# The residual h goes straight into the output, and the last rows are added to it by accumulating transfers from GpSimd

## The chip, the core and the metric

The kernel runs on one core of a Trainium2 chip. The metric is the time of one execution on the device in microseconds. Three runs of the kernel before gave 2551.84, 2552.77 and 2554.0 us, median 2552.77 us. The profiled execution has a span of 2550.6 us from its first to its last instruction.

Engine names in the rows are those of the profiler: PE is TensorE (PEld its weight loads), DVE is VectorE, ACT is ScalarE, POOL is GpSimd, SP is SyncE. ACTq is ScalarE's own issuing of transfers.

## The reference, cut to what matters

One layer of a decoder over 512 prompt rows and 64 sample rows, with D_MODEL = 2048:

```
xn = rmsnorm(x, n_mix_pre);  mix = mixer(xn)          # GLA and SSD heads, one output projection
h  = x + rmsnorm(mix, n_mix_post)
xn = rmsnorm(h, n_ffn_pre);  f = conv_ffn(xn)         # FFN_DIM = 5632, causal depthwise conv, silu gate
y  = h + rmsnorm(f, n_ffn_post)
```

All is float32. The outputs are y and the recurrent and convolution states. Only the last line is touched by the change: how h is kept from its making to the final addition, and who adds it.

## The kernel before, in words

Data are held with the model dimension on the partitions: 2048 features are KT = 16 tiles of 128, and a tile has T = 576 columns (512 prompt rows and 64 sample rows). Many steps work on half a tile, HALF = 288 columns; n = 0 and n = 1 name the halves. Nothing is scheduled by a library: every engine has its own program, written out in order, and waits on semaphores. An instruction that waits holds everything behind it on its engine.

Three stages matter here.

**Making h.** At about 940 to 980 us GpSimd adds x to the normalised mixer output (`add_x`, L555), and ScalarE scales and squares the result (`h_high`, L1006 and L1009). In the second half (n = 1), after every second tile, ScalarE issues one transfer of two tiles of h to the DRAM tensor `h_spill` (L1011, 8 transfers of 576 KB). VectorE waits for all of them (L2652) before it normalises h in place. In the down projection ScalarE issues one load of all of h (4608 KB) back into `x_hi` (L1255), at 2370.8 us.

**The last sums.** The down projection runs over five chunks of the FFN dimension; the last (`last_down`) gives 32 half tiles, first the 16 of n = 0 and then the 16 of n = 1. VectorE adds each to `acc` (`take_last`, L2775). ScalarE squares it (L1272) into a ring of four buffers, and the squares are summed over the tiles by two engines, tiles 1, 3, 4, 6, 7, 9, 10, 12 by GpSimd (`square_sum`, L579) and 5, 8, 11, 13, 14 by VectorE (L2795). The square of tile kt waits for the sum of tile kt-4. When all sums of a half are done, TensorE adds across partitions (`tokens_squared`, L1906), ScalarE takes the root (L1260, L1262), VectorE the reciprocal (L2446, L2448), and TensorE spreads it over the partitions (`roots_to_rows`, L1914).

**The last rows.** VectorE multiplies each half tile by its norm (`y_of`, L2784): those of n = 0 between the takes of n = 1, from 2519.4 us, and those of n = 1 after 2536.7 us. Then h is added, in SBUF: by VectorE for three tiles of n = 0 and five of n = 1 (`VE_ADDS`, L2787), by GpSimd for the other 24 half tiles (`add_h`, L586). ScalarE issues the stores to `yT` (`rows_out`, L1284), four for n = 0 and five for n = 1, seven of 576 KB and two of 288 KB. In its program they all stand behind the second root. At the end it waits for the nine stores (`y_st`, 144 = 9 x 16).

Of the kernel before, what the change touches and what calls it, by code (L numbers as in the profile page):

```python
# [30 lines left out]
F32 = mybir.dt.float32  # L31
F32R = mybir.dt.float32r
U8 = mybir.dt.uint8
ALU = mybir.AluOpType
# [3 lines left out]
P = 128  # L38
# [3 lines left out]
T = SEQ + SMP  # L42
KT = D // P
# [66 lines left out]
    _n += _w  # L110
NVEC = _n
MASK_TRI, MASK_TRI_S = 8, 9
VE_ADDS = ((7, 11, 15), (3, 7, 11, 14, 15))
POOL_SUMS, VE_SUMS = (1, 3, 4, 6, 7, 9, 10, 12), (5, 8, 11, 13, 14)

PADW = SC - 1 + SEQ + BATCHES * (SC - 1 + DEC)
# [13 lines left out]
def build(nc, xT, weights, vecs, ident_d, masks_d, gate2, sconv_in, fconv_in, fvec_d, gla_in,  # L130
          ssdT_in, ssd_in, yT, gla_p, ssd_p, sconv_out, fconv_out, gla_s, ssd_s):
    y_spill = nc.dram_tensor("y_spill", [2, 8, P, T], F32, kind="Internal").ap()
    spill = nc.dram_tensor("spill", [BESIDE, P, T], F32, kind="Internal").ap()
    h_spill = nc.dram_tensor("h_spill", [KT, P, T], F32, kind="Internal").ap()
    g_spill = nc.dram_tensor("g_spill", [FT, P, T], F32, kind="Internal").ap()
    with ExitStack() as ctx:
        def sb(name, shape, dt=F32):
# [2 lines left out]
        def sem(name):  # L140
            return ctx.enter_context(nc.semaphore(name))
# [126 lines left out]
        def h_pair(j):  # L268

            at = 1152 * (7, 2, 3, 4, 5, 6, 1, 0)[j]  # L270
            return A(at, 1152)
# [77 lines left out]
        setup = sem("setup")  # L349
        own_step = sem("own_step")  # L350
        sc_in, pad_st, qk_in, y_kept, ylo = (sem(n) for n in ("sc_in", "pad_st", "qk_in", "y_kept", "ylo"))
        h_m, y_m, added_p, added_v = (sem(n) for n in ("h_m", "y_m", "added_p", "added_v"))
        ysq_sum, ysq_vsum = sem("ysq_sum"), sem("ysq_vsum")
        yb_in = [sem("yb_in%d" % i) for i in range(4)]
        vec_in, masks_in = sem("vec_in"), sem("masks_in")
# [40 lines left out]
        x_sum, op_high, op_low = (sem(n) for n in ("x_sum", "op_high", "op_low"))  # L396
        ws_ready, whs_ready, wl_ready = (sem(n) for n in ("ws_ready", "whs_ready", "wl_ready"))
        p1_out, g_st = sem("p1_out"), sem("g_st")
        h_back, y_st = sem("h_back"), sem("y_st")

        block = ctx.enter_context(nc.Block())

# [63 lines left out]
        def cut(ap, n):  # L466

            return ap[:, n * HALF:(n + 1) * HALF]
# [49 lines left out]
        @block.gpsimd  # L518
        def _(pool):

            def weight_lo(unit, slot, r):
                pool.wait_ge(hi_ready, unit + 1)
                nc.gpsimd.tensor_tensor(w_lo[:, slot], raw[:, r], w_hi[:, slot].bitcast(F32),  # L523
                                        ALU.subtract).then_inc(lo_ready, 1)

            weight_lo(0, 0, 0)
            weight_lo(1, 1, 1)

            def weights_lo(start, stop):

                with pool.Fori(start, stop) as i:
                    for j in range(4):
                        weight_lo(4 * i + 2 + j, (2 + j) % 4, j % 2)

            at_ynorm, at_h = (GAP_YNORM // 2 + N_TILE0 + 2) // 2, (FFN_UNIT0 + 4 - 2) // 4
            weights_lo(0, at_ynorm)

            for j in range(2):
                weight_lo(4 * at_ynorm + 2 + j, 2 + j, j)
            for j in range(4):  # L540
                pool.wait_ge(yhi, j + 1)
                nc.gpsimd.tensor_tensor(XC[:, j], XC[:, j], yh[:, j], ALU.subtract).then_inc(ylo, 1)
            for j in range(2):
                weight_lo(4 * at_ynorm + 4 + j, j, j)
            weights_lo(at_ynorm + 1, at_h - 1)

            def std_lo(j):
                weight_lo(FFN_UNIT0 + j, (2 + j) % 4, j % 2)

            def add_x(n, kt):  # L550

                pool.wait_ge(h_m, KT * n + kt + 1)
                pool.wait_ge(block_in[kt // 4], 64 if kt >= 12 else 16)
                h = cut(h_of(kt), n)
                nc.gpsimd.tensor_tensor(h, h, cut(xres(kt), n), ALU.add).then_inc(added_p, 1)  # L555

            std_lo(0)
            add_x(0, 0)
            add_x(0, 1)
            std_lo(1)  # L560
            for kt in range(2, 8):
                add_x(0, kt)
            std_lo(2)
            for kt in range(8, 11):
                add_x(0, kt)
            std_lo(3)
            for kt in range(11, KT):
                add_x(0, kt)
            for kt in range(KT):
                add_x(1, kt)  # L570
            std_lo(4)
            std_lo(5)
            def square_sum(n, kt):

                pool.wait_ge(squared, Y_SQUARES0 + KT * n + kt + 1)
                done = POOL_SUMS.index(kt)
                if n or done:
                    pool.wait_ge(ysq_sum, len(POOL_SUMS) * n + done)
                nc.gpsimd.tensor_tensor(cut(fsum, n), cut(fsum if done else fsq[0], n), cut(fsq[kt % 4], n),  # L579
                                        ALU.add).then_inc(ysq_sum, 1)  # L580

            def add_h(n, kt):

                pool.wait_ge(y_m, KT * n + kt + 1)
                a = cut(acc[:, kt], n)
                nc.gpsimd.tensor_tensor(a, a, cut(x_hi[:, kt ^ 1].bitcast(F32), n), ALU.add).then_inc(added_p, 1)  # L586

            for kt in POOL_SUMS:
                square_sum(0, kt)
            pool.wait_ge(h_back, 16)  # L590
            adds = [kt for kt in range(KT) if kt not in VE_ADDS[0]]
            for kt, first, stop in ((1, 0, 0), (3, 0, 0), (4, 0, 1), (6, 1, 1), (7, 1, 2), (9, 2, 2), (10, 2, 3),
                                    (12, 3, len(adds))):
                square_sum(1, kt)
                for j in range(first, stop):
                    add_h(0, adds[j])
            for kt in range(KT):
                if kt not in VE_ADDS[1]:
                    add_h(1, kt)


        @block.scalar
        def _(act):
# [398 lines left out]
            def h_high(n, kt):  # L1002

                act.wait_ge(added_p, KT * n + kt + 1)
                h = cut(h_of(kt), n)
                nc.scalar.activation(cut(x_std(kt, 0), n), h, ACT.Copy, scale=V("ffn_pre", kt)).then_inc(op_high, 1)  # L1006
                if kt >= 2:
                    act.wait_ge(hsq_mm, KT * n + kt - 1)
                nc.scalar.activation(cut(sq[kt % 2], n), h, ACT.Square).then_inc(h_squared, 1)  # L1009
                if n and kt % 2:  # L1010
                    act.dma_start(h_spill[kt - 1:kt + 1].rearrange("n p t -> p n t"),  # L1011
                                  h_pair(kt // 2).rearrange("p (n t) -> p n t", n=2)).then_inc(h_st, 16)

            for e in range(HALF_TILES):
                mix_square(e)
# [223 lines left out]
            for v in range(4, DOWN_UNITS):  # L1239
                hi_down(v)  # L1240
                if v == CHUNK_V0[1] + 3:
                    for batch in (7, 8, 9):
                        g_load(batch)
                if v == CHUNK_V0[2] + 3:
                    for batch in (10, 11, 12, 13):
                        g_load(batch)
                for q in high_after.get(v, ()):
                    g_high(q)
                if v == CHUNK_V0[3] - 2:
                    for batch in (14, 15):  # L1250
                        g_load(batch)
                    for q in (FT - 2, FT - 1):
                        g_high(q)
                if v == CHUNK_V0[3] + 3:
                    act.dma_start(x_hi[:].bitcast(F32), h_spill.rearrange("n p t -> p n t")).then_inc(h_back, 16)  # L1255

            def root_of_tokens(n):

# [16 lines left out]
                        root_of_tokens(0)  # L1275
            root_of_tokens(1)

            def rows_out(n, first, stop):

                by_ve = sum(kt < stop for kt in VE_ADDS[n])  # L1280
                act.wait_ge(added_v, len(VE_ADDS[0]) * n + by_ve)
                act.wait_ge(added_p, 2 * KT + (KT - len(VE_ADDS[0])) * n + stop - by_ve)
                i, a = divmod(first, 4)
                act.dma_start(yT[i, :, a:a + stop - first, n * HALF:(n + 1) * HALF],  # L1284
                              acc[:, first:stop, n * HALF:(n + 1) * HALF]).then_inc(y_st, 16)

            for i in range(4):
                rows_out(0, 4 * i, 4 * i + 4)
            for i in range(3):
                rows_out(1, 4 * i, 4 * i + 4)  # L1290
            rows_out(1, 12, 14)
            rows_out(1, 14, 16)
            act.wait_ge(y_st, 144)
            act.wait_ge(fo_st, 16)
            act.wait_ge(sconv_st, 16)
# [636 lines left out]
        def _(ve):  # L1932
# [716 lines left out]
            take_std(0, 1)  # L2649
            std_low(6)  # L2650
            std_low(7)
            ve.wait_ge(h_st, 128)  # L2652
            for j in range(4):
                normalise(j)
            taps_of(0, 0)
# [121 lines left out]
            def y_of(n, kt):  # L2777

                if kt == 0:
                    ve.wait_ge(ysq_mm, 2 * n + 2)  # L2780
                    ve.wait_ge(h_back, 16)
                    ve.wait_ge(squared, Y_SQUARES0 + KT * (n + 1))
                a = cut(acc[:, kt], n)
                stt(a, a, V("ffn_post", kt), work[:, n, 0:HALF], ALU.mult, ALU.mult).then_inc(y_m, 1)  # L2784
                if kt in VE_ADDS[n]:
                    ve.wait_ge(y_m, KT * n + kt + 1)
                    tt_op(a, a, cut(x_hi[:, kt ^ 1].bitcast(F32), n), ALU.add).then_inc(added_v, 1)  # L2787

            def square_sum(n, kt):

# [135 lines left out]
```

## Time and profile before

| | |
|---|---|
| median of three runs | 2552.77 us |
| span of the profiled execution | 2550.6 us |
| TensorE busy | 2500.4 us, 98% of the span |
| VectorE busy | 1662.6 us, 65% |
| ScalarE busy | 932.0 us, 37% |
| GpSimd busy | 391.3 us, 15% |
| granted TensorE clock, mean | 0.993 |

The time of the profiled execution outside its span is not shown by the profile; the median of the runs is 2.2 us above the span. Busy shares are means over the whole program. TensorE has its last matmul of the down projection at 2526.6 us, so 24 us at the end are set by other things, and it is there that the change works.

### The profile page before, as it was taken

The numbers are of one execution on the slowest core, as the hardware profiler recorded it, in microseconds if no ns is written. First come the engines' busy times: TensorE is split into PE (matmuls) and PEld (weight loads), VectorE is DVE, ScalarE is ACT, GpSimd is POOL, SyncE is SP. The second block draws the span as 40 slices with busy tenths as digits, with TensorE's granted clock in tenths as the row PEclk, the third lists the DMA queues.
The fourth block names the chain that finished last, engine by engine and source line by source line (L and its number), as shares of the span: only waits on it lengthen the run. The fifth ranks groups of instructions, "written<-read, shape, count | busy, mean of one in ns | idle before, by whom it ended". The sixth has DMA issues, their size and how long they took to land. (4 is left out here: it accounts for less than half of the span.)

```text
span 2550.6 us, 48785 instructions
## 1 busy us (share of the span) xinstructions
PE 2500.4 (98%) x20582; PEld 2469.2 (97%) x20582; DVE 1662.6 (65%) x2395; ACT 932.0 (37%) x1324; POOL 391.3 (15%) x208
## 2 busy tenths in 40 slices
PE   7999999999999999999999999999999999999997
PEld 7999999999999999999999999999999999999997
DVE  6544555765146368899999999999998333333226
ACT  5332223423214245444444444444445222122112
POOL 3333222433233352000000000000000000000005
PEclk9999999999999999999999999999999999999998
DMA  4223237622373424233333333333335423333422
GB/s 178 85 82 96 73 116 259 215 78 77 112 253 103 157 67 149 86 98 113 106 114 105 109 106 114 106 113 106 114 107 176 142 76 129 91 123 97 157 84 85
DMA packets 97415, 303.32 MB, mean 119 GB/s; under 512 B 10160, under 2 KB 14896, under 8 KB 96320
## 3 DMA queue, kind: packets, MB, share of 16 engines
q1 hardware_dynamic: 58336, 211.84, 27.0%
q10 hardware_dynamic: 38880, 88.59, 9.6%
q8 instruction: 153, 2.51, 0.4%
q14 instruction: 46, 0.38, 0.0%
HBM read 255.77 MB, written 44.62 MB: 118 GB/s over the span
## 5 line engine op out<-in xcount | busy, mean ns | idle before, releaser
L1311 PE MATMUL psum_proj<-x_hi,w_hi 128*128 128x288 f32 (+2 forms) x1696 | 510.8, 301 | 15.1 <-DVE x_lo L1957 13.1
L1311 PE MATMUL psum_proj<-x_lo,w_hi 128*128 128x288 f32 (+2 forms) x1696 | 501.1, 295 | 0.0
L1313 PE MATMUL psum_proj<-x_hi,w_lo 128*128 128x288 f32 (+2 forms) x1696 | 500.7, 295 | 0.0
L523 POOL TENSOR_TENSOR w_lo<-raw,w_hi 128x1024 fp32r<-128x1024 f32 x128 | 321.3, 2513 | 620.2 <-ACT w_hi L609 620.2
L1311 PEld LDWEIGHTS psum_proj<-x_hi,w_hi 128*128 128x128 f32 x1696 | 320.7, 189 | 22.4 <-issue 15.6
L1311 PEld LDWEIGHTS psum_proj<-x_lo,w_hi 128*128 128x128 f32 x1696 | 319.9, 189 | 2.7 <-issue 1.9
L609 ACT ACTIVATE w_hi<-raw 128x1024 fp32r<-128x1024 f32 x138 | 145.2, 1056 | 484.3 <-PE psum_proj L1313 410.2
L1313 PEld LDWEIGHTS psum_proj<-x_hi,w_lo 128*128 128x128 f32 x1696 | 319.6, 188 | 0.0
L1812 PE MATMUL psum_proj<-ops_a,w_hi 128*128 128x288 f32 x890 | 262.5, 295 | 2.5 <-DVE w_lo L2638 2.0
L1814 PE MATMUL psum_proj<-ops_a,w_lo 128*128 128x288 f32 x890 | 262.1, 294 | 0.0
L1813 PE MATMUL psum_proj<-ops_a,w_hi 128*128 128x288 f32 x890 | 261.9, 294 | 0.0
L1812 PE MATMUL psum_work<-ops_a,w_hi 128*128 128x288 f32 x876 | 258.0, 295 | 0.8 <-DVE w_lo L2638 0.8
L1814 PE MATMUL psum_work<-ops_a,w_lo 128*128 128x288 f32 x876 | 258.0, 295 | 0.0
L1813 PE MATMUL psum_work<-ops_a,w_hi 128*128 128x288 f32 x876 | 257.8, 294 | 0.0
L1121 ACT ACTIVATE w_hi<-raw 128x1024 fp32r<-128x1024 f32 x88 | 93.3, 1061 | 421.8 <-PE psum_work L1814 213.2
L579 POOL TENSOR_TENSOR arena<-arena 128x288 f32<-128x288 f32 x16 | 13.1, 821 | 1526.2 <-ACT arena L1272 1525.2
L984 ACT ACTIVATE w_hi<-tail 128x1024 fp32r<-128x1024 f32 x106 | 112.6, 1062 | 200.2 <-DVE tail L2428 200.1
L1812 PEld LDWEIGHTS psum_proj<-ops_a,w_hi 128*128 128x128 f32 x890 | 167.0, 188 | 3.4 <-DVE w_lo L2638 2.5
L1812 PE MATMUL psum_proj<-ops_b,w_hi 128*128 128x288 f32 x568 | 168.4, 297 | 0.2 <-DVE x_flat L2595 0.2
L1812 PE MATMUL psum_work<-ops_b,w_hi 128*128 128x288 f32 x558 | 165.2, 296 | 3.0 <-DVE w_lo L2439 3.0
L1814 PE MATMUL psum_proj<-ops_b,w_lo 128*128 128x288 f32 x568 | 167.9, 296 | 0.0
L1813 PE MATMUL psum_proj<-ops_b,w_hi 128*128 128x288 f32 x568 | 167.8, 295 | 0.0
(421 smaller groups left out, 6319.0 us busy)
## 6 DMA issues: line engine op xcount, KB each, us to landing
raw<-in_weights_dram SPq DMA_DIRECT2D x386, 512.0 KB, 3.6
g_spill<-x_flat ACTq DMA_DIRECT2D x44, 288.0 KB, 2.2
spill<-tail ACTq DMA_DIRECT2D x24, 288.0 KB, 2.1
arena<-in_xT_dram SPq DMA_DIRECT2D x4, 1152.0 KB, 10.7
y_spill<-arena ACTq DMA_DIRECT2D x4, 1152.0 KB, 5.1
h_spill<-arena ACTq DMA_DIRECT2D x8, 576.0 KB, 2.9
x_hi<-h_spill ACTq DMA_DIRECT2D x1, 4608.0 KB, 18.7
x_flat<-g_spill ACTq DMA_DIRECT2D x5, 864.0 KB, 9.0
```

The source lines that it names most:

```text
L523: nc.gpsimd.tensor_tensor(w_lo[:, slot], raw[:, r], w_hi[:, slot].bitcast(F32), ALU.subtract).then_inc(lo_ready, 1)
L579: nc.gpsimd.tensor_tensor(cut(fsum, n), cut(fsum if done else fsq[0], n), cut(fsq[kt % 4], n), ALU.add).then_inc(ysq_sum, 1)
L609: nc.scalar.activation(w_hi[:, slot], raw[:, r], ACT.Copy).then_inc(hi_ready, 1)
L984: nc.scalar.activation(w_slot(w, 0)[:, 6:14], w_sum, ACT.Copy).then_inc(whs_ready, 1)
L1121: nc.scalar.activation(w_hi[:, (2 + v) % 4], raw[:, v % 2], ACT.Copy).then_inc(hi_ready, 1)
L1311: nc.tensor.matmul(banks[:, n, 0:b - a], w_hi[:, slot, k], (hi, lo)[part][:, a:b], start=first and part == 0, stop=False)
L1313: mm = nc.tensor.matmul(banks[:, n, 0:b - a], w_lo[:, slot, k], hi[:, a:b], start=False, stop=last)
L1812: nc.tensor.matmul(to, w_h, hi, start=first, stop=False)
L1813: nc.tensor.matmul(to, w_h, lo, start=False, stop=False)
L1814: return nc.tensor.matmul(to, w_l, hi, start=False, stop=last)
```

## The change

h is stored during its making into the output tensor `yT` itself, tile by tile (16 transfers of 288 KB from ScalarE, in the place of 8 of 576 KB to `h_spill`). `h_spill` and the load of it into `x_hi` are gone, and so are all 32 additions of h in SBUF, on VectorE (8) and on GpSimd (24). The nine transfers of final rows are issued by GpSimd in place of ScalarE, with `accum_op=ADD`: each adds the rows in `acc` to what stands in `yT`. Two of them stand between GpSimd's sums of squares, seven behind.

```diff
-VE_ADDS = ((7, 11, 15), (3, 7, 11, 14, 15))
...
-            def add_h(n, kt):
-
-                pool.wait_ge(y_m, KT * n + kt + 1)
-                a = cut(acc[:, kt], n)
-                nc.gpsimd.tensor_tensor(a, a, cut(x_hi[:, kt ^ 1].bitcast(F32), n), ALU.add).then_inc(added_p, 1)
+            def add_to_h(n, first, stop):
+
+                pool.wait_ge(y_m, KT * n + stop)
+                i, a = divmod(first, 4)
+                pool.dma_start(yT[i, :, a:a + stop - first, n * HALF:(n + 1) * HALF],
+                               acc[:, first:stop, n * HALF:(n + 1) * HALF], accum_op=ALU.add).then_inc(y_st, 16)
...
-            pool.wait_ge(h_back, 16)
-            adds = [kt for kt in range(KT) if kt not in VE_ADDS[0]]
-            for kt, first, stop in ((1, 0, 0), (3, 0, 0), (4, 0, 1), (6, 1, 1), (7, 1, 2), (9, 2, 2), (10, 2, 3),
-                                    (12, 3, len(adds))):
+            pool.wait_ge(h_st, 16 * KT)
+            for kt in POOL_SUMS:
                 square_sum(1, kt)
-                for j in range(first, stop):
-                    add_h(0, adds[j])
-            for kt in range(KT):
-                if kt not in VE_ADDS[1]:
-                    add_h(1, kt)
+                if kt in (4, 9):
+                    add_to_h(0, 4 * (kt // 5), 4 * (kt // 5) + 4)
+            for first, stop in ((8, 12), (12, 16)):
+                add_to_h(0, first, stop)
+            for first, stop in ((0, 4), (4, 8), (8, 12), (12, 14), (14, 16)):
+                add_to_h(1, first, stop)
...
-                if n and kt % 2:
-                    act.dma_start(h_spill[kt - 1:kt + 1].rearrange("n p t -> p n t"),
-                                  h_pair(kt // 2).rearrange("p (n t) -> p n t", n=2)).then_inc(h_st, 16)
+                if n:
+                    act.dma_start(yT[kt // 4, :, kt % 4, :], h_of(kt)).then_inc(h_st, 16)
...
-                if v == CHUNK_V0[3] + 3:
-                    act.dma_start(x_hi[:].bitcast(F32), h_spill.rearrange("n p t -> p n t")).then_inc(h_back, 16)
...
-            def rows_out(n, first, stop):
-
-                by_ve = sum(kt < stop for kt in VE_ADDS[n])
-                act.wait_ge(added_v, len(VE_ADDS[0]) * n + by_ve)
-                act.wait_ge(added_p, 2 * KT + (KT - len(VE_ADDS[0])) * n + stop - by_ve)
-                i, a = divmod(first, 4)
-                act.dma_start(yT[i, :, a:a + stop - first, n * HALF:(n + 1) * HALF],
-                              acc[:, first:stop, n * HALF:(n + 1) * HALF]).then_inc(y_st, 16)
-
-            for i in range(4):
-                rows_out(0, 4 * i, 4 * i + 4)
-            for i in range(3):
-                rows_out(1, 4 * i, 4 * i + 4)
-            rows_out(1, 12, 14)
-            rows_out(1, 14, 16)
...
-            ve.wait_ge(h_st, 128)
+            ve.wait_ge(h_st, 16 * KT)
...
-                    ve.wait_ge(h_back, 16)
                     ve.wait_ge(squared, Y_SQUARES0 + KT * (n + 1))
                 a = cut(acc[:, kt], n)
                 stt(a, a, V("ffn_post", kt), work[:, n, 0:HALF], ALU.mult, ALU.mult).then_inc(y_m, 1)
-                if kt in VE_ADDS[n]:
-                    ve.wait_ge(y_m, KT * n + kt + 1)
-                    tt_op(a, a, cut(x_hi[:, kt ^ 1].bitcast(F32), n), ALU.add).then_inc(added_v, 1)
```

GpSimd's last rows before. L579 are the sums of squares of n = 1, from tile 1 in the first row to tile 12 in the last but one; L586 are the additions of h. In brackets stand the semaphores waited for.

```order
L579 TENSOR_TENSOR arena<-arena 128x288 [waits ysq_sum,squared,h_back]
L579 TENSOR_TENSOR arena<-arena 128x288 [waits ysq_sum,squared] x2
L586 TENSOR_TENSOR arena<-arena,x_hi 128x288 [waits y_m]
L579 TENSOR_TENSOR arena<-arena 128x288 [waits ysq_sum,squared] x2
L586 TENSOR_TENSOR arena<-arena,x_hi 128x288 [waits y_m]
L579 TENSOR_TENSOR arena<-arena 128x288 [waits ysq_sum,squared] x2
L586 TENSOR_TENSOR arena<-arena,x_hi 128x288 [waits y_m]
L579 TENSOR_TENSOR arena<-arena 128x288 [waits ysq_sum,squared]
L586 TENSOR_TENSOR arena<-arena,x_hi 128x288 [waits y_m] x21
```

The same place in the changed kernel, where L577 are the sums and L584 the accumulating transfers:

```order
L577 TENSOR_TENSOR arena<-arena 128x288 [waits ysq_sum,squared,h_st]
L577 TENSOR_TENSOR arena<-arena 128x288 [waits ysq_sum,squared] x2
L584 DMA out_yT_dram<-arena 512x1x288 [waits y_m]
L577 TENSOR_TENSOR arena<-arena 128x288 [waits ysq_sum,squared] x3
L584 DMA out_yT_dram<-arena 512x1x288 [waits y_m]
L577 TENSOR_TENSOR arena<-arena 128x288 [waits ysq_sum,squared] x2
L584 DMA out_yT_dram<-arena 512x1x288 [waits y_m] x5
L584 DMA out_yT_dram<-arena 128x2x288 [waits y_m] x2
```

The first addition, behind the sum of tile 4, waited for one product of n = 0; the transfer that now stands there waits for four. The second transfer waits for eight and stands before the sums of tiles 10 and 12. All nine transfers now stand in GpSimd's order.

VectorE's last rows before: L2784 are the products with the norm, L2787 the additions of h, the two reciprocals belong to n = 1.

```order
L2784 SCALAR_TENSOR_TENSOR arena<-arena,vec,psum_work 128x288 x3
L2446 RECIPROCAL rstd<-rstd 128x2
L2448 RECIPROCAL rstd<-rstd 32x1
L2784 SCALAR_TENSOR_TENSOR arena<-arena,vec,psum_work 128x288
L2787 TENSOR_TENSOR arena<-arena,x_hi 128x288
L2784 SCALAR_TENSOR_TENSOR arena<-arena,vec,psum_work 128x288 x4
L2787 TENSOR_TENSOR arena<-arena,x_hi 128x288
L2784 SCALAR_TENSOR_TENSOR arena<-arena,vec,psum_work 128x288 x4
```

And in the changed kernel, where L2763 are the products, up to the end of the program:

```order
L2763 SCALAR_TENSOR_TENSOR arena<-arena,vec,psum_work 128x288
L2755 TENSOR_TENSOR arena<-psum_proj,arena 128x288
L2771 TENSOR_TENSOR arena<-arena 128x288
L2763 SCALAR_TENSOR_TENSOR arena<-arena,vec,psum_work 128x288 x5
L2426 RECIPROCAL rstd<-rstd 128x2
L2428 RECIPROCAL rstd<-rstd 32x1
L2763 SCALAR_TENSOR_TENSOR arena<-arena,vec,psum_work 128x288 x17
```

The 16 products of n = 1 now follow one another, behind the last product of n = 0; nothing else moved on VectorE.

## Rows read from the trace of the kernel before

**Rows 1.** The page: busy time of each engine.
```profile
PE 2500.4 (98%) x20582; PEld 2469.2 (97%) x20582; DVE 1662.6 (65%) x2395; ACT 932.0 (37%) x1324; POOL 391.3 (15%) x208
```

**Rows 2.** Busy time by stretch at the end; last columns clock, DMA share, GB/s.
```profile
2531.00:2534.30 3.30, 3.22 (x19) 3.22 (x20) 2.94 (x6) 0.09 (x1) 3.30 (x5) 0.50 0.00 0
2538.50:2547.00 8.50, 0.00 (x0) 0.00 (x0) 8.17 (x18) 0.00 (x0) 8.03 (x10) 0.50 0.95 324
2547.00:2549.00 2.00, 0.00 (x0) 0.00 (x0) 0.00 (x0) 0.00 (x0) 0.00 (x0) 0.50 1.00 322
2549.00:2550.00 1.00, 0.00 (x0) 0.00 (x0) 0.00 (x0) 0.00 (x0) 0.00 (x0) 0.50 0.68 232
2550.00:2550.60 0.60, 0.00 (x0) 0.00 (x0) 0.00 (x0) 0.00 (x0) 0.00 (x0) 0.50 0.00 0
```

**Rows 3.** DMA queues and issues, 2515 to 2552 us (37 us).
```profile
q10 hardware_dynamic: 4240, 4.72, 37.5%
...
out_yT_dram<-arena ACTq DMA_DIRECT2D x7, 576.0 KB, 4.2
out_yT_dram<-arena ACTq DMA_DIRECT2D x2, 288.0 KB, 2.9
```

**Rows 4.** VectorE in order of time: start, us, line, operation, idle before.
```profile
2522.60 0.50 DVE L2784 SCALAR_TENSOR_TENSOR arena<-arena,vec,psum_work 128x288 f32<-128x288 f32 x1
...
2526.49 0.51 DVE L2784 SCALAR_TENSOR_TENSOR arena<-arena,vec,psum_work 128x288 f32<-128x288 f32 x1
...
2529.98 1.00 DVE L2795 TENSOR_TENSOR arena<-arena 128x288 f32<-128x288 f32 x1
2530.90 0.93 DVE L2784 SCALAR_TENSOR_TENSOR arena<-arena,vec,psum_work 128x288 f32<-128x288 f32 x2
...
2534.78 0.48 DVE L2784 SCALAR_TENSOR_TENSOR arena<-arena,vec,psum_work 128x288 f32<-128x288 f32 x1
...
2536.73 1.79 DVE L2784 SCALAR_TENSOR_TENSOR arena<-arena,vec,psum_work 128x288 f32<-128x288 f32 x4 [0.81 <-PE psum_work L1914]
2538.55 0.63 DVE L2787 TENSOR_TENSOR arena<-arena,x_hi 128x288 f32<-128x288 f32 x1
...
2546.34 0.51 DVE L2787 TENSOR_TENSOR arena<-arena,x_hi 128x288 f32<-128x288 f32 x1
```

**Rows 5.** GpSimd in order of time.
```profile
2517.05 1.74 POOL L579 TENSOR_TENSOR arena<-arena 128x288 f32<-128x288 f32 x2 [2.59 <-ACT arena L1272]
...
2521.71 1.76 POOL L579 TENSOR_TENSOR arena<-arena 128x288 f32<-128x288 f32 x2 [0.93 <-ACT arena L1272]
...
2527.19 1.01 POOL L579 TENSOR_TENSOR arena<-arena 128x288 f32<-128x288 f32 x1
```

**Rows 6.** ScalarE and its queue in order of time.
```profile
2524.66 0.45 ACT L1272 ACTIVATE arena<-arena 128x288 f32<-128x288 f32 x1 [0.71 <-DVE arena L2775]
...
2528.74 0.44 ACT L1272 ACTIVATE arena<-arena 128x288 f32<-128x288 f32 x1 [0.35 <-DVE arena L2775]
...
2534.28 0.64 ACTq L1284 DMA_DIRECT2D out_yT_dram<-arena  x1
```

**Rows 7.** TensorE in order of time, the norm of n = 1.
```profile
2531.08 3.10 PE L1906 MATMUL psum_work<-ones,arena 128*128 128x1 f32 x18 [3.06 <-DVE arena L2795]
```

**Rows 8.** The stores' issue on ScalarE's queue: least, median and longest ns.
```profile
L1284 ACTq DMA_DIRECT2D out_yT_dram<-arena x9: 391/542/1357, 2534.3 to 2547.1; - x9
```

**Rows 9.** GpSimd's costliest group in the whole span.
```profile
L523 POOL TENSOR_TENSOR w_lo<-raw,w_hi 128x1024 fp32r<-128x1024 f32 x128 | 321.3, 2513 | 620.2 <-ACT w_hi L609 620.2
```

**Rows 10.** DMA queues in the 20 us from 2370, with the load of h.
```profile
q10 hardware_dynamic: 2064, 4.72, 62.0%
```

**Rows 11.** Busy time by stretch, where h is stored and loaded.
```profile
985.00:1010.00 25.00, 25.00 (x193) 25.00 (x192) 23.33 (x34) 11.44 (x16) 0.00 (x0) 1.00 0.42 127
2370.00:2390.00 20.00, 20.00 (x153) 20.00 (x152) 5.77 (x6) 3.19 (x3) 0.00 (x0) 1.00 0.89 320
```

**Rows 12.** The stores of h, and the first use of h's place after.
```profile
L1011 ACTq DMA_DIRECT2D h_spill<-arena x8: 366/366/393, 957.2 to 978.6; - x8
...
991.25 0.81 DVE L2534 SCALAR_TENSOR_TENSOR arena<-arena,vec,rstd 128x576 f32<-128x576 f32 x1
```

**Rows 13.** DMA issues of single tiles and pairs elsewhere: KB, us to landing.
```profile
h_spill<-arena ACTq DMA_DIRECT2D x8, 576.0 KB, 2.9
...
arena<-spill ACTq DMA_DIRECT2D x1, 576.0 KB, 4.0
```

More of the change, by code:

```diff
@@ L133, in build @@
     spill = nc.dram_tensor("spill", [BESIDE, P, T], F32, kind="Internal").ap()
-    h_spill = nc.dram_tensor("h_spill", [KT, P, T], F32, kind="Internal").ap()
     g_spill = nc.dram_tensor("g_spill", [FT, P, T], F32, kind="Internal").ap()
@@ L351, in build @@
         sc_in, pad_st, qk_in, y_kept, ylo = (sem(n) for n in ("sc_in", "pad_st", "qk_in", "y_kept", "ylo"))
-        h_m, y_m, added_p, added_v = (sem(n) for n in ("h_m", "y_m", "added_p", "added_v"))
+        h_m, y_m, added_p = (sem(n) for n in ("h_m", "y_m", "added_p"))
         ysq_sum, ysq_vsum = sem("ysq_sum"), sem("ysq_vsum")
@@ L398, in build @@
         p1_out, g_st = sem("p1_out"), sem("g_st")
-        h_back, y_st = sem("h_back"), sem("y_st")
+        y_st = sem("y_st")
         block = ctx.enter_context(nc.Block())
```

## The prediction

> **What bounds the kernel now.** I read the page first: TensorE is busy for 98% of the span [rows 1], so an edit pays only where TensorE is not what ends a stage. Then the stretches around the three places that the change touches. Where h is stored and where it is loaded back, TensorE is busy for 25.00 of 25 us and 20.00 of 20 us [rows 11]; both are covered. The end is different: TensorE's last work is the norm of n = 1, and from 2538.5 to 2547 it has nothing, VectorE is busy for 8.17 of 8.5 us, GpSimd for 8.03, and the DMA engines for 95% at 324 GB/s [rows 2]. So the last 14 us have three nearly equal limits: VectorE's products and additions, GpSimd's additions, and the stores. The stores are dense because none is issued before 2534.28 [rows 6], 15 us after the first product; from there 4.72 MB go out. VectorE ends at 2546.85, the last bytes move until about 2549.7 (0.68 of the last busy microsecond), and 0.9 us later the span ends [rows 2, 4].
>
> **The change, part by part.**
>
> Making h: 16 issues in the place of 8, each 0.37 us on ScalarE's queue [rows 12], beside the activations. If all eight new ones stood in the way, that would be 8 x 0.37 = 3.0 us of ScalarE, spread over 20 us in which TensorE has matmuls; the last store is issued at 978.6, takes 2.9 us to land [rows 12, 13], and h is first overwritten at 991.25 [rows 12], 9.7 us after. I take 0; without the cover it would be up to 3. The load of h in the down projection disappears beside a full TensorE [rows 11]: 0.
>
> VectorE at the end: five additions leave the chain of n = 1. Four products take 1.79 us together with their overlap, 0.43 each, so 16 take 6.9 us; before, the stretch from 2536.73 to 2546.85 took 10.1 us [rows 4]. The last product is done at 2543.6 in place of 2546.3, and by itself this is worth 3.2 us. GpSimd's 24 additions go too, so its sums and the transfers are all that it does.
>
> The new work is nine accumulating transfers on GpSimd. No row shows one. Two prices are needed.
>
> Price G, GpSimd's time to issue one of 576 KB, in which its queue stands still. The nearest row is ScalarE's issue of the same transfer, median 0.54 us [rows 8]. The other row that I have is GpSimd's longest operation in this trace, 2.5 us [rows 9]. The ends are 0.54 and, should the addition's two sources cost it one such time each, 5 us. I take 1.5, between the two rows, and half for the two small ones. In the Trainium skill, "DMA: Bandwidth & Descriptors", section "SWDGE vs HWDGE vs iDMA", a transfer from GpSimd has its descriptors made by software, and the page's specifications give about 1 us to the first byte against 0.6 from ScalarE. No run here shows it; by 1 us in place of 1.5 the sum would not change, since the transfers behind set the end.
>
> Price R, the time in which the 16 engines move one such transfer. A plain store is the lower end: 4.72 MB took 37.5% of 37 us [rows 3], 13.9 us or 1.73 us for one eighth, which is one large transfer. The accumulating one must also fetch the old rows from DRAM. The load of the same 4.72 MB took 62.0% of 20 us [rows 10], 12.4 us or 1.55 for an eighth. If the engines take the two in turn, R = 1.73 + 1.55 = 3.3 us. The upper end is that fetch and write of one transfer do not overlap with the next: 4.0 us for a load to land and 4.2 for a store [rows 3, 13], 8.2 together. I take 3.3, the value in which every byte is counted once in each direction.
>
> In the Trainium skill, "Collectives: The Full Stack", section "The bandwidth ceiling: the fold count and why AG ≠ RS ≠ AR", an adding transfer is said to run at half the rate of a copy (62.28 to 32.35 GB/s) because it reads two sources. No row here bears on it; an estimate by that page's ratio is 1.73 x 1.93 = 3.3 us, and the sum would be the same.
>
> Now the walk, with products ready as before. The products are ready for transfer 1 at 2523.1, for 2 at about 2527.5 (product 7 starts at 2526.49, and ahead of it VectorE's sum of tile 11 hangs on GpSimd's sum of tile 7, which moves), for 3 at 2531.8, for 4 at 2535.3 [rows 4]. With G = 1.5:
> - Transfer 1 moves 2524.6 to 2527.9, transfer 2 from 2529.1 to 2532.4, transfer 3 from 2533.3 to 2536.6, transfer 4 from 2536.8 to 2540.1.
> - n = 1: products 0 to 3 are ready at 2538.5, issue done at 2540.0. From here the engines never idle: 2543.4, 2546.7, 2550.0, then the two small ones 2551.65 and 2553.3. GpSimd issues the last of them near 2545, so the transfers set the end.
> - The same 0.9 us from last byte to end: 2554.2, against 2550.6. That is +3.6 us.
>
> Does transfer 1 delay the norm? It stands before the sums of tiles 6 and 7, which ran from 2521.71 to 2523.47 [rows 5]. Now GpSimd waits for product 3 until 2523.1, issues until 2524.6, and sums tile 6 by 2525.4, 7 by 2526.2, 9 by 2527.0. The square of tile 10 started at 2524.66 [rows 6] and now starts at 2525.4; transfer 2 holds GpSimd to about 2529.2, the sum of tile 10 ends at 2530.0, the square of tile 14 (2528.74 before) starts there, and VectorE's last sum ends at about 2530.9, where it ended at 2530.98 [rows 4]. GpSimd's last ends at 2530.8; before it was 2528.2 [rows 5]. So at G = 1.5 the slack is used up and the norm starts at 2531.1 as before [rows 7]; every microsecond of G beyond delays it by one or more.
>
> The sum: 0 + 0 + 3.6. The profiled execution has no time of its own beside the span; the median is 2.2 us above the span, and I keep that: 2552.77 + 3.6 = 2556.4 us.
>
> **The rivals.**
>
> Faster side: the fetch of the old rows is hidden in the store, R = 1.73. For it speaks that reads and writes of a transfer are different work and that a load ran at 4.72 MB in 12.4 us [rows 10], faster than the store; against it, that the stores already keep the engines at 95 to 100% [rows 2]. Then n = 0 is out before n = 1 begins, transfer 5 moves 2540.0 to 2541.7, 6 to 2543.4, 7 from 2543.4 to 2545.1, the small ones to 2546.9, end 2547.8: -2.8 us, 2550.0. This is all that the removed additions can give.
>
> Slower side, the issue: GpSimd's in-order queue becomes the bound. It decides from G = 1.5 on. At G = 2.5 [rows 9] the sums of tiles 10 and 12 end at 2531.8 and 2532.6, the norm starts 1.6 us late, the products of n = 1 with it, and the last issue ends near 2550; with R = 3.3 the walk gives 2556.8, +6.2, so 2559.0. At G = 5 the norm is 6.6 us late, and nine issues one behind another end at 2567.6; with 1.65 for the last transfer and 0.9, +19.6, so 2572.4. For it: five sums and two blocking waits stand in one queue with the issues [rows 5]. Against it: ScalarE's issue takes 0.54 [rows 8].
>
> Slower side, the transfer: the fetches are not overlapped. At R = 5 eight units from 2524.6 give 2564.6 and 0.9, +14.9, so 2567.7; at 8.2 they give +40.5, 2593. For it speaks only that a 576 KB load or store alone takes 4.0 and 4.2 us to land [rows 3, 13].
>
> **How the numbers follow.** The forecast (R of two passes, G up to 1.7) has 0.45, with 2553.5 to 2559.5 as its own range; R near a plain store 0.23; a slow issue 0.20; a slow transfer 0.12. 0.2% is 5.1 us, about what a measurement tells from no change: 2547.7 to 2557.9 is the same. Of the forecast 0.32 falls within it and 0.13 above; of the fast rival 0.19 within and 0.04 below; of the slow issue 0.02 within and 0.18 above; the slow transfer is above. So faster 0.04, same 0.53, slower 0.43. The range runs from a little below the fast rival to a little above the slow issue at G = 5: 2549.3 to 2573; what lies outside is mainly the slow transfer beyond R = 5.5.
>
> **What would show it.** The duration of GpSimd's transfers in its queue gives G; the DMA share and GB/s from 2540 on give R, with a full share and half of the 324 GB/s (if the writes alone are counted) for my value. The products of n = 1 should run from about 2536.7 to 2543.6 without a gap. The matmuls of the second norm should start within 0.5 us of 2531.1. The stretches at 985 and 2370 should have TensorE full as before. I am wrong if the last bytes move less than 3 us after the last product (then R is that of a store), or if GpSimd's queue, not the transfers, is busy to the end.

## The result, and the profile after

| | before | changed |
|---|---|---|
| median of ten runs | 2553.27 us (2550.15 to 2554.67) | 2557.75 us (2555.67 to 2560.49) |
| ratio, 95% interval | | 1.002 (1.0011 to 1.0028) |
| span of the profiled execution | 2550.6 us | 2557.4 us |
| VectorE's first product of n = 0 | 2519.38 | 2521.39 |
| tail, from there to the end of the span | 31.2 us | 36.0 us |

The change makes the kernel 0.2% slower, 4.5 us in the medians; I had said 3.6. That is inside the 0.2% (5.1 us) within which the prediction called a time the same, while the interval excludes 1. The two profiled spans differ by more, 6.8 us, and 2.0 of that is there before the tail begins. It need not be the change's: two executions of one and the same program (e9 and e12 below) had their first product at 2517.70 and 2521.36. So I compare tails. They differ by 4.8 us, about what the medians differ by.

GpSimd in order of time in the changed kernel (L577 the sums, L584 the accumulating transfers), which answers to [rows 5]:

```profile
2519.07 1.75 POOL L577 TENSOR_TENSOR arena<-arena 128x288 f32<-128x288 f32 x2 [2.58 <-ACT arena L1267]
2524.96 1.35 POOL L584 DMA_DIRECT2D out_yT_dram<-arena  x1 [4.15 <-DVE arena L2763]
2525.81 3.25 POOL L577 TENSOR_TENSOR arena<-arena 128x288 f32<-128x288 f32 x3
2530.11 1.22 POOL L584 DMA_DIRECT2D out_yT_dram<-arena  x1 [1.04 <-DVE arena L2763]
2530.84 2.30 POOL L577 TENSOR_TENSOR arena<-arena 128x288 f32<-128x288 f32 x2
...
2541.64 1.21 POOL L584 DMA_DIRECT2D out_yT_dram<-arena  x1 [2.04 <-DVE arena L2763]
2543.34 1.21 POOL L584 DMA_DIRECT2D out_yT_dram<-arena  x1 [0.49 <-DVE arena L2763]
2545.04 3.65 POOL L584 DMA_DIRECT2D out_yT_dram<-arena  x3 [0.49 <-DVE arena L2763]
```

An issue takes 1.2 us, the first 1.35. Before the first one GpSimd stands still for 4.15 us; it waits for product 3, and three sums stand behind it. All nine are issued by 2548.7, and GpSimd then has nothing: the end is not its.

VectorE, which answers to [rows 4], and TensorE's sum over partitions for n = 1, which answers to [rows 7]:

```profile
2521.39 0.51 DVE L2763 SCALAR_TENSOR_TENSOR arena<-arena,vec,psum_work 128x288 f32<-128x288 f32 x1
...
2539.55 6.89 DVE L2763 SCALAR_TENSOR_TENSOR arena<-arena,vec,psum_work 128x288 f32<-128x288 f32 x16 [1.47 <-PE psum_work L1894]
```

```profile
2533.90 3.10 PE L1886 MATMUL psum_work<-ones,arena 128*128 128x1 f32 x18 [3.87 <-ACT arena L1267]
```

The sixteen products of n = 1 take 6.89 us without a gap. They start 18.16 us after the first product (17.35 before), and the span ends 17.85 us after their start (13.87 before). The 4.8 us are thus 0.8 + 4.0.

Busy time by stretch; the last columns are granted clock, DMA share, GB/s, as in [rows 2]. The third is short of the end by 2.4 us.

```profile
2540.00:2545.00 5.00, 0.00 (x0) 0.00 (x0) 5.00 (x13) 0.00 (x0) 2.41 (x2) 0.50 1.17 163
2545.00:2550.00 5.00, 0.00 (x0) 0.00 (x0) 1.44 (x4) 0.00 (x0) 3.65 (x3) 0.50 1.21 194
2550.00:2555.00 5.00, 0.00 (x0) 0.00 (x0) 0.00 (x0) 0.00 (x0) 0.00 (x0) 0.50 1.22 196
```

VectorE is done at 2546.44 and GpSimd at 2548.7, and the DMA engines go on alone at 196 GB/s, against 324 before. The share adds up the time of every packet, so a share over 1 means that packets overlap in time on an engine. In 40 slices of 1.1 us from 2515, the same shows as a flat stretch:

```profile
DMA  0000000000399917998499999999999999999500
GB/s 0 0 0 0 0 0 0 7 0 15 17 109 183 200 27 41 159 200 136 30 123 196 191 111 184 201 157 178 199 188 198 197 193 195 198 198 198 84 0 0
```

At 198 GB/s a transfer of 590 kB takes 2.98 us. The gaps before 2541 are the engines' waits for the next transfer of n = 0.

The two covered places stayed covered, as in [rows 11]. TensorE's 24.56 us of 25 hold a wait of 0.4 us that fell before 985 us in the other execution:

```profile
985.00:1010.00 25.00, 24.56 (x188) 24.30 (x187) 23.25 (x30) 8.79 (x14) 3.08 (x2) 1.00 0.44 136
2370.00:2390.00 20.00, 20.00 (x153) 20.00 (x152) 6.40 (x7) 3.92 (x4) 0.00 (x0) 1.00 0.31 97
```

### The profile page after: what moved, and what is told of

Its sections match the earlier page's. It is cut to its first block and busy times, and to the rows that moved or that the text cites. A ratio compares the mean times of both kernels' runs of the same rounds, so it can differ in the third digit from the quotient of the medians.

```text
span 2557.4 us, 48751 instructions
## 1 busy us (share of the span) xinstructions
PE 2502.7 (98%) x20582; PEld 2471.3 (97%) x20582; DVE 1656.6 (65%) x2387; ACT 932.5 (36%) x1324; POOL 381.8 (15%) x193
## 3 DMA queue, kind: packets, MB, share of 16 engines
q0 software_dynamic: 4240, 4.72, 1.2%
## 5 line engine op out<-in xcount | busy, mean ns | idle before, releaser
L1291 PE MATMUL psum_proj<-x_hi,w_hi 128*128 128x288 f32 (+2 forms) x1696 | 510.0, 301 | 15.7 <-DVE x_lo L1937 13.6
L577 POOL TENSOR_TENSOR arena<-arena 128x288 f32<-128x288 f32 x16 | 14.0, 876 | 1524.3 <-ACT arena L1267 1523.1
L1794 PEld LDWEIGHTS psum_proj<-ops_a,w_lo 128*128 128x128 f32 x890 | 167.1, 188 | 0.0
```

The costliest lines, as they stand in the source:

```text
L1291: nc.tensor.matmul(banks[:, n, 0:b - a], w_hi[:, slot, k], (hi, lo)[part][:, a:b], start=first and part == 0, stop=False)
L1794: return nc.tensor.matmul(to, w_l, hi, start=False, stop=last)
```

## The experiments

In all of them I read three numbers from the profile: where n = 1's products start, counted from n = 0's first product; what passes from there to the end; and the sum, the tail. Each tail is that of one profiled execution; the two of one program (e9 and e12) differ by 0.4 us.

| run | start of n = 1 | from there to the end | tail | median, ratio to before (interval) |
|---|---|---|---|---|
| before | 17.35 | 13.87 | 31.2 | |
| changed | 18.16 | 17.85 | 36.0 | 2557.75, 1.002 (1.0011 to 1.0028) |
| e1_copy | 17.12 | 12.4 | 29.5 | 2550.07, 0.9987 (0.9978 to 0.9996) |
| e4_act_copy | 15.20 | 13.2 | 28.4 | 2549.7, 0.9987 (0.9978 to 0.9996) |
| e5_second_only | 14.38 | 17.84 | 32.2 | 2554.51, 1.0008 (0.9999 to 1.0017) |
| e2_tiles | 17.36 | 13.9 | 31.3 | 2552.69, 0.9998 (0.9989 to 1.0007) |
| e8_late | 15.43 | 18.5 | 34.0 | 2554.49, 1.0007 (0.9998 to 1.0016) |
| e9_half_late | 15.28 | 13.9 | 29.2 | 2551.04, 0.9991 (0.9982 to 1.0) |
| e12_again (e9 once more) | 14.95 | 13.9 | 28.8 | 2550.69, 0.9995 (0.9986 to 1.0004) |
| e10_quarter_late | 14.83 | 14.7 | 29.6 | 2551.99, 0.9992 (0.9983 to 1.0001) |
| e13_half_behind | 14.61 | 15.3 | 29.9 | 2551.19, 0.9997 (0.9988 to 1.0006) |
| e11_rows | 14.69 | 27.5 | 42.1 | 2564.32, one run |

### e1: the same transfers as copies

```diff
-                               acc[:, first:stop, n * HALF:(n + 1) * HALF], accum_op=ALU.add).then_inc(y_st, 16)
+                               acc[:, first:stop, n * HALF:(n + 1) * HALF]).then_inc(y_st, 16)
```

> The changed kernel with the addition taken out of its nine last transfers: GpSimd issues the same transfers in the same order as plain copies, so the rows written are f's part alone, without h. I measure the tail, from VectorE's first product of n = 0 to the end of the span: 31.2 us before, 36.0 changed. Theory A (the addition sets the rate of the transfers, 2.98 us each where a copy takes 1.73): the engines fall back to 1.7 us a transfer, the last issue is then the limit, tail about 29 us, 7 us less than changed and 2 less than before. Theory B (it is the issue by GpSimd that makes the transfers slow, whoever adds): tail stays near 36, and the rate near 198 GB/s. GpSimd's issue, 1.22 us each in the changed kernel: A has no view on it; if the addition costs a second description it falls below 1.

Tail 29.5 us, 6.5 less than changed. GpSimd's issues, by group (count, busy, mean ns, idle before), and its DMA queue in the 44 us from 2515:

```profile
L584 POOL DMA_DIRECT2D out_yT_dram<-arena x9 | 6.6, 732 | 14.5 <-DVE arena L2763 14.2
```

```profile
q0 software_dynamic: 1168, 4.72, 30.8%
```

The same queue in the changed kernel over the same 44 us:

```profile
q0 software_dynamic: 4240, 4.72, 72.4%
```

30.8% of 44 us is 13.6 us, 1.7 us a transfer, as when ScalarE issued them before (13.9 us). The accumulation raises that to 31.9 us of engine time. Theory B falls: GpSimd's copies move as fast as ScalarE's stores, so the addition sets the rate. The copy also went out in fewer packets, 1168 for 4240. That is not what makes it fast: ScalarE's stores in e4 below went out in 4240 and took 14.1 us. From n = 1's first product to the end the addition costs 17.85 - 12.4 = 5.4 us. It also makes the issue longer (1.22 against 0.73 us), and that, twice among the sums, fits the 1.0 us by which the start of n = 1 moves.

### e4: nobody adds, ScalarE stores

```diff
-                if kt in (4, 9):
-                    add_to_h(0, 4 * (kt // 5), 4 * (kt // 5) + 4)
...
+            def rows_out(n, first, stop):
+                act.wait_ge(y_m, KT * n + stop)
...
+                act.dma_start(yT[i, :, a:a + stop - first, n * HALF:(n + 1) * HALF],
+                              acc[:, first:stop, n * HALF:(n + 1) * HALF]).then_inc(y_st, 16)
```

> The changed kernel without its nine accumulating transfers: ScalarE issues nine plain stores behind the second root, where the kernel before has them, and nobody adds h (left out). It shows what the removed additions alone are worth. Theory A: no block in GpSimd's sums, the norm starts as in the kernel before or a little earlier, products of n = 1 done 3.2 us earlier; the stores cannot start before the root, so 4.72 MB at 340 GB/s set the end: tail 14.9 + 13.9 + 0.9 = 29.7 us, 1.5 less than before. Rival (VectorE's chain set the end before, the stores were hidden): tail 31.2 - 3.2 = 28.0 us.

Tail 28.4 us, between the two expectations. The stores did queue: q10 moved its 4.72 MB in 14.1 us. But the products of n = 1 started 2.1 us earlier than before, more than the "little earlier" of theory A. TensorE's row:

```profile
2530.37 2.56 PE L1893 MATMUL psum_work<-ones,arena 128*128 128x1 f32 x18 [1.44 <-ACT arena L1261]
```

It starts 10.1 us after the first product (11.7 before [rows 7]) and takes 2.56 us in place of 3.10. So all the additions together are worth 2.8 us of tail, 0.11% of the kernel, and more than half of it is an earlier norm and not a shorter chain at the end.

### e5: without the transfers of n = 0

```diff
-                if kt in (4, 9):
-                    add_to_h(0, 4 * (kt // 5), 4 * (kt // 5) + 4)
-            for first, stop in ((8, 12), (12, 16)):
-                add_to_h(0, first, stop)
...
-            act.wait_ge(y_st, 144)
+            act.wait_ge(y_st, 80)
```

> The changed kernel without the four accumulating transfers of n = 0 (those rows of the output stay at h); the five of n = 1 are as they are. Theory A: n = 0's transfers are over before those of n = 1 can start, they cost only the 0.8 us by which the two in GpSimd's queue delay the norm: tail 36.0 - 0.8 = 35.2 us. Rival (all eight units queue one behind another, the end is set by the sum of them): the end comes 3 us or more earlier, tail 33 or less.

I expected 35.2 and got 32.2. By the number alone the rival had won, yet its mechanism had not: from n = 1's first product to the end it takes 17.84 us, the same as with n = 0's transfers (17.85). In this order they do not lengthen the queue at all. The whole 3.8 us stand ahead of it, in the norm:

```profile
2527.74 1.28 PE L1897 MATMUL psum_proj<-ident,ones 128*128 128x128 f32 x10
2530.45 1.75 PE L1882 MATMUL psum_work<-ones,arena 128*128 128x1 f32 x18 [1.43 <-ACT arena L1263]
```

```profile
2530.40:2532.20 1.80, 1.75 (x19) 1.75 (x19) 1.80 (x5) 0.00 (x0) 0.00 (x0) 0.99 0.00 0
2532.20:2534.70 2.50, 2.49 (x9) 1.85 (x8) 0.75 (x4) 0.40 (x2) 0.00 (x0) 0.50 0.00 0
```

The stretch of the changed kernel that holds the same eighteen matmuls:

```profile
2533.90:2537.00 3.10, 3.10 (x19) 3.07 (x19) 1.87 (x5) 0.00 (x0) 1.22 (x1) 0.50 0.83 116
```

The matmuls start 10.07 us after the first product, not 12.51: 2.4 us were GpSimd's blocked sums. And they take 1.75 us in place of 3.10, another 1.35: after 1.4 us of idling TensorE still ran at 0.99 of its clock, that is 2.4 GHz, and after the 3.9 us of idling in the changed kernel it ran at 0.50, 1.2 GHz. The wait is paid for twice. How much the second time varies: after the same 1.44 us of idling the row took 2.56 us in e4, where the clock fell within it, so an early norm gives back between 0.5 and 1.35 us here.

### e2: h stored in 16 pieces

The kernel before, with h stored as below; each addition now reads the load's tile kt in place of kt ^ 1, since the tiles no longer lie in swapped pairs.

```diff
-                if n and kt % 2:
-                    act.dma_start(h_spill[kt - 1:kt + 1].rearrange("n p t -> p n t"),
-                                  h_pair(kt // 2).rearrange("p (n t) -> p n t", n=2)).then_inc(h_st, 16)
+                if n:
+                    act.dma_start(h_spill[kt], h_of(kt)).then_inc(h_st, 16)
```

> The kernel before with one edit: h is stored to its own tensor tile by tile, 16 transfers of 288 KB in the place of 8 of 576 KB; load and additions as before. Theory A: no difference, ratio 1.000 within 0.001, and TensorE as busy from 940 to 1010 us as before. Rival: the eight more issues stand in ScalarE's way, up to 8 x 0.37 = 3 us, ratio 1.001.

No difference (0.9998), as priced. The interval, 0.09% to each side, would hide 2 us; the tail is unchanged, and TensorE is busy for 67.6 of the 70 us from 940, against 67.5 before.

### e8: nothing that waits among the sums

```diff
             for kt in POOL_SUMS:
                 square_sum(1, kt)
-                if kt in (4, 9):
-                    add_to_h(0, 4 * (kt // 5), 4 * (kt // 5) + 4)
-            for first, stop in ((8, 12), (12, 16)):
+                if kt == 7:
+                    add_to_h(0, 0, 4)
+            for first, stop in ((4, 8), (8, 12), (12, 16)):
                 add_to_h(0, first, stop)
```

> The changed kernel with the two accumulating transfers that stand among GpSimd's sums moved so that they wait for nothing there: the first behind the sum of tile 7, the second behind the sum of tile 12. Without n = 0's transfers the products of n = 1 started 14.4 us after the first product of n = 0, in the changed kernel 18.2, in the kernel before 17.4. Theory A (two causes: the blocked sums hold up the norm, and 2.98 us a transfer sets the rest): the norm starts about 10.1 to 10.6 us after the first product, its matmuls run partly at the higher clock (1.8 to 2.6 us in place of 3.1), tail 32.2 to 33.2 in place of 36.0, still 1 to 2 us more than before (31.2). Rival (the norm's delay is not GpSimd's, and n = 0's transfers now run into n = 1's): tail 35 or more.

```profile
2523.82 1.35 POOL L584 DMA_DIRECT2D out_yT_dram<-arena  x1
2524.67 2.30 POOL L577 TENSOR_TENSOR arena<-arena 128x288 f32<-128x288 f32 x2
```

The first transfer now waits for nothing, and the sums behind it follow at once. n = 1 starts 2.7 us earlier than changed, and the tail is 2.0 us shorter, 34.0; the expected 32.2 to 33.2 missed by most of a microsecond, as n = 0's transfers, issued later, seem to run into n = 1's (18.5 us to the end in place of 17.85). So the order cost the change about 2 us, and the rate of accumulation the rest: this is still 2.8 us longer than before.

### e11: longer pieces

```diff
+            for first in range(0, KT, 2):
+                pool.wait_ge(y_m, KT + first + 2)
+                i, a = divmod(first, 4)
+                pool.dma_start(yT[i, :, a:a + 2], acc[:, first:first + 2], accum_op=ALU.add).then_inc(y_st, 16)
```

> Measures the rate of accumulation with longer rows: eight accumulating transfers of two whole tiles each (4608 B a partition in one piece, where the changed kernel has pieces of 1152 B), all behind the second norm; sums and products as changed, the same 4.72 MB. Theory A (an accumulation reads twice and writes once, bytes count): 2.98 us a transfer, 198 GB/s, as with short pieces, from first to last about 24 us. Rival (the pieces count, each has a fixed price): well above 230 GB/s and under 20 us. GpSimd's issue: 1.2 us if it goes by transfers, under 0.8 if by pieces.

One run, of 2564.32 us; it is this long because no row leaves before 2537.5. The DMA engines in the 32 us from 2530:

```profile
DMA  0000000008779999999999999999999999999980
GB/s 0 0 0 0 0 0 0 0 0 75 69 138 207 196 207 202 207 207 213 219 207 196 219 207 213 213 213 213 213 202 219 207 219 207 213 213 213 207 161 0
```

About 210 GB/s in place of 198: pieces four times as long give 6%, and from first to last it takes 24 us as theory A has it. So a fixed price of each piece is not what makes accumulation slow. GpSimd's eight issues took 7.26 us, 0.91 each against 1.21, so the issue does depend on the pieces, which fitted neither number.

### e9 and e12: accumulate where there is time, add in SBUF where there is none

The transfers of n = 0 stand as in e8; h's half of n = 1 is stored to a tensor of its own, loaded as before and added by VectorE and GpSimd, and ScalarE stores the sums. The 32 half tiles of h are stored one by one. BY_DMA is 0. The edit where h is made (the load, the additions and the plain stores of n = 1 stand as in the kernel before and are left out here):

```diff
-                if n:
-                    act.dma_start(yT[kt // 4, :, kt % 4, :], h_of(kt)).then_inc(h_st, 16)
+                if n == 0 or kt < BY_DMA:
+                    act.dma_start(yT[kt // 4, :, kt % 4, n * HALF:(n + 1) * HALF], h).then_inc(h_st, 16)
+                else:
+                    act.dma_start(h_spill[kt], h).then_inc(h_st, 16)
```

> n = 0 by accumulating transfers in the places of e8_late; n = 1 as in the kernel before: h's second half is stored apart, loaded into SBUF in the down projection, added there by VectorE (tiles 3, 7, 11, 14, 15) and GpSimd, and stored plain by ScalarE. Theory A: n = 0's transfers are out before n = 1's stores, the norm is early, and from n = 1's first product to the end it takes what it took before or less, 12.9 to 13.9 us: tail 27.5 to 28.5, 3 us less than before, ratio about 0.999. Rival (the transfers of n = 0 overlap with n = 1's stores and slow them, or 32 stores of h cost ScalarE time): tail 31 or more, ratio 1.000.

The DMA engines in e9, in 40 slices of 1.1 us from 2515:

```profile
DMA  0000000799999999999999594999200000000000
GB/s 0 0 0 0 7 15 0 49 126 201 160 59 167 200 154 124 190 195 195 200 238 352 177 330 133 322 323 326 72 0 0 0 0 0 0 0 0 0 0 0
```

The four accumulating transfers run at up to 200 GB/s under the sums, the norm and the first products of n = 1, and are over when the plain stores come at 320 to 350. Tail 29.2 us, 2.0 less than before. I had expected 27.5 to 28.5. The rest of n = 1 (13.9 us) was within what I had said; its start was not, 15.28 where I had counted on about 14.6. The interval of the ratio, 0.9991, touches 1.

> The kernel of e9_half_late once more, for a second interval: there ratio 0.9991 (0.9982 to 1.0), tail 29.2 us against 31.2 before. If the tail's 2 us are real the ratio is again 0.9988 to 0.9996; if e9's gain was chance it is 1.000 or above.

The tail is 2.4 us shorter than before, and the ratio 0.9995, inside the expected 0.9988 to 0.9996, but with an interval over 1. Both executions show the tail shorter; that the whole kernel is faster is not shown.

### e10 and e13: two variants

e10 sets BY_DMA to 4, so that tiles 0 to 3 of n = 1 accumulate too.

> As e9_half_late, but tiles 0 to 3 of n = 1 go by an accumulating transfer too, and the other twelve are added in SBUF (VectorE 7, 11, 14, 15). Theory A: the engines have the room, VectorE and GpSimd have 12 additions for 16; tail 26.9 to 28, at best 1 us less than e9_half_late. Rival (that transfer, 2.98 us, pushes the plain stores behind it): 1 us more than e9_half_late.

The start is 0.1 to 0.5 us earlier and the rest 0.8 longer than in e9 and e12: VectorE needs 0.8 us more for n = 1, and one of its additions took 2.32 us beside GpSimd's, where the others take 0.5 to 1.1. The tail of 29.6 gives nothing. e13 puts all four transfers of n = 0 behind the sums.

```diff
-                if kt in (4, 9):
-                    add_to_h(0, 4 * (kt // 5), 4 * (kt // 5) + 4)
-            for first, stop in ((8, 12), (12, 16)):
+            for first, stop in ((0, 4), (4, 8), (8, 12), (12, 16)):
```

> As e9_half_late, but all four accumulating transfers of n = 0 stand behind GpSimd's sums. Theory: nothing but sums stands among the sums, so the norm starts 10.1 us after the first product (10.4 in e9) and n = 1's products 14.4 (15.3 in e9), but the four transfers of 2.98 us start about 4 us later, end near 21 us after the first product and run into n = 1's stores: tail 28.3 to 29.5. Rival (the collision costs more than the earlier norm gives): 30 or more.

The norm's matmuls start 10.1 us after the first product and n = 1's products at 14.61, as expected; the collision eats it, 15.3 us to the end, tail 29.9, between the two expectations. By the tails (29.2 and 28.8 against 29.9) one transfer among the sums, where its products are ready, is the better place; by the medians nothing can be told.

## Why the prediction was right, and where it was off

- **Where the time goes.** The forecast had the accumulating transfers of n = 1, one behind another, setting the end, and the medians 3.6 us up; they went 4.5 up. e1 shows the cause: without the addition the end comes 5.4 us sooner after n = 1's first product.
- **R, the price of one transfer.** Taken as a store and a load in turn, 3.3 us; measured 2.98 us at 198 GB/s, within 10%. There is some luck in this. I had worked R out from busy time of the engines, and in busy time a transfer takes 31.9 / 8 = 4.0 us, a fifth more than 3.3. It passes in 2.98 because the packets overlap (share 1.2), which I had not reckoned with. My sign, half of 324 GB/s, was 198, that is 0.61. The fast rival (1.73) is what e1 measures for the copy. That the price is the fetch of the old rows, and not the adding itself or the wait for the rows, was argued from the load's row and fits; no run separates them.
- **From n = 1's first product to the end** the walk gave 17.5 us (2536.7 to 2554.2), and 17.85 was measured, by two errors that cancel. Four units at 2.98 are 1.3 us less than at 3.3. But about 1.6 us pass in e5 from the beginning of the first issue (2536.87) to the first bytes, where I let them move at the end of a 1.5 us issue and at full rate; the rate takes about another microsecond to come up; 0.34 us lie between product and issue; and from the last bytes to the end it is 1.1 us, not 0.9.
- **G, the issue.** Taken as 1.5, measured 1.2. The slow-issue rival, at 2.5 us or more, was out.
- **The norm.** This is the step that failed: "at G = 1.5 the slack is used up and the norm starts at 2531.1 as before". It started 0.8 us later (12.51 us after the first product, 11.70 before), with a shorter issue than assumed, and outside the 0.5 us that I had named as a sign. It is most of what the forecast lacks: the walk's tail is 34.8 us, the measured one 36.0. The walk holds up to the square of tile 14, 10.9 us after the first product where I had 10.6. Then I let VectorE's sum of tile 14 end it. What TensorE waited for was the square of tile 15. It came late because VectorE's sum of tile 13 took 1.60 us beside GpSimd's sum behind transfer 2, against 1.10 in e1 with its shorter issue and 0.44 in e8, and VectorE's take of tile 15 stands behind it; the profile's chain of work runs through these rows:

```profile
2530.89 1.60 DVE L2771 TENSOR_TENSOR arena<-arena 128x288 f32<-128x288 f32 x1
...
2532.83 0.45 DVE L2755 TENSOR_TENSOR arena<-psum_proj,arena 128x288 f32<-128x288 f32 x1
...
2533.31 0.44 ACT L1267 ACTIVATE arena<-arena 128x288 f32<-128x288 f32 x1 [0.62 <-DVE arena L2755]
```

- **The comparison with before.** I asked only whether the blocked sums came later than before. e5 shows that the removal of the additions alone would have let the norm start 1.6 us earlier, and with the clock still up. Against that, the two transfers in GpSimd's queue cost 3.8 us in these executions. The wait for product 3 (4.15 us) uses up the slack, and behind it the issues count in full: in e1 they are 0.5 us shorter each, and the norm starts 1.0 us earlier. In e8, where nothing waits there, the one issue left among the sums costs 0.3 us against e5, and moving two lines takes back 2.7 us of the start. The slow-issue rival thus had a part of the mechanism right at a price below the 1.5 us from which it was to decide.
- **VectorE's five additions** were worth what I said: 16 products in 6.89 us. In the changed kernel they seem to buy nothing, since the transfers behind are longer; no run tests this.
- **The middle of the kernel** was priced at nothing. e2 finds nothing above its 0.09%, and TensorE stays full at 2370 us without the load [rows 11].

In the Trainium skill, the page "Collectives: The Full Stack", section "The bandwidth ceiling: the fold count and why AG ≠ RS ≠ AR", has the reducing step between cores at half the rate of the copying one, since it reads two sources. Here, for a transfer within one core, the rate falls from 340 to 198 GB/s, to 0.58, and with longer pieces to 0.62. The measurement decides: a little better than half.

## What to carry to other kernels

An accumulating transfer moves an addition from engines that compute to the DMA engines, at about 1.7 times the DMA time of a plain store. It costs little where the DMA engines idle (e9, e12), and is dear at the very end, where nothing else is left to hide it (e1, e8). When it is put in an in-order queue, place it behind the last producer it needs, not where the first is ready: the wait for its data holds up whatever stands behind. And when an edit removes work, price the new wait against the schedule without that work, not against the old one.

## What the runs showed that I had not expected

- The same eighteen one-column matmuls took 1.75, 1.88, 1.98, 2.01, 2.05, 2.34, 2.47, 2.56 or 3.10 us in these runs. In e5 the granted clock during them was 0.99, in the changed kernel 0.50; the 3.10 is that of the kernel before too, at 0.50 [rows 2, 7]. TensorE had idled 1.4 to 1.8 us before the shorter ones and 2.8 to 3.9 us before the 3.10. Among the shorter ones the idling does not decide: one program took 2.34 (e9) and 2.01 (e12) after 1.75 and 1.74 us, with the clock falling within the row.
- GpSimd's issue of the same 590 kB took 0.73 us as a copy and 1.22 as an accumulation, and the copy went out in 1168 packets where the accumulation, and ScalarE's store before, took 4240. Which of the two makes its issue shorter, the missing second source or the fewer packets, is open; with 4608 B pieces the accumulation had 1152 packets and 0.91 us.
- From 940 to 960 us the granted clock was 1.00 in the profiles of before and e9 and 0.83 in all others, among them e12, which is e9's program. In that stretch TensorE did 120 matmuls in the first two and 98 to 100 in the others. The tail begins at 2519.38 and 2517.70 us in the first two, and between 2519.62 and 2521.39 in the others; e2, at 0.83, began only 0.2 us later than before, so the clock there is not shown to be the cause. This is noise of the size of the effect under study, and the reason to compare tails.
